# Loading the first expert group's up projection as whole matrices instead of quarters of four experts, in a one-core encoder kernel

## The chip, the core and the metric

The kernel runs on one core of one Trainium2 chip. It is written by hand, with explicit semaphores, for TensorE (PE in the profile), VectorE (DVE), ScalarE (ACT), GpSimd (POOL) and SyncE (SP), which here does little but issue DMA loads of weights. The metric is the device time of one execution in microseconds (us). Before the change it is 1241.25 us, the median of three runs (1240.59, 1241.25, 1242.27).

## The reference

A two-layer encoder trunk works on 256 tokens of width 1024, in float32. Each layer has a token mixer (neighbourhood attention in layer 0, gated linear attention in layer 1) beside a small memory attention, then an output projection, then a mixture of experts. The part that matters here is the mixture:

```
g_gate, g_idx = lax.top_k(g_prob, 1)             # one of 4 groups per token
top_l, top_i = lax.top_k(e_logits, TOP_K)        # two of its 8 experts
gate = softmax(top_l) * g_gate
...
def expert_block(args):
    xi, e = args
    return (jax.nn.silu(xi @ w1[e]) * (xi @ w3[e])) @ w2[e]
```

There are 32 experts in a layer. w1 and w3 of an expert are 1024 x 512, w2 is 512 x 1024, each 2 MB in float32. All of them are read in each layer, 192 MB a layer.

## The kernel before

**Groups of four experts.** The kernel walks the experts of a layer in 8 groups (NQ = 8) of four (E4 = 4), and gives each expert 32 rows of a 128-row tile. For each group `quad` on TensorE gathers the tokens by a matmul with a selection matrix (L644), multiplies them by w1 and then by w3 (both L657, the function `up`; m = 0 is w1, the "up projection" of the change, and m = 1 is w3), transposes the activation (L686), multiplies by w2 (L661, `down`) and adds the result back to the tokens (L712). Each float32 matmul is two instructions in the profile, so that w1 or w3 of one group is 64 rows on L657, and w2 is 64 rows on L661.

**The ring.** The weights go through a ring of 10 slots in SBUF, 2 MB each (SLOTS = 10). A group needs 12 fills: fills 0 to 3 for w1, 4 to 7 for w3, 8 to 11 for w2. SyncE issues the fills strictly in order (`experts` in the SyncE block, `load`, L434). Fills 0 to 9 of a layer go to slots that the mixer before has used, each behind its own condition (`free0`, `free1`). Fill n from the tenth on waits until TensorE has counted up `ring_used` for fill n - 10 (`free`, L422). So the last two fills of the first group, 10 and 11, which are half of its w2, go to the slots in which its fills 0 and 1 were. In the text "fill 10" means the eleventh fill of a layer.

**Two layouts of a fill.** If a matrix is "sliced" in a group, one fill holds a quarter of the rows of all four experts, in runs of 4 KB (tile 128x4x1024). If not, a fill is one expert's whole matrix, in runs of 16 KB (tile 128x4096). With sliced w1 TensorE waits for one fill, does 16 rows of matmul with it, counts `ring_used` up by one, and goes to the next. With whole w1 it waits for all four fills (L668), goes through all 64 rows with the four experts in turn, and counts the four fills as used at the last eight rows, where k is 7. The table `SLICED` says for each of the 8 groups which matrices are sliced, and holds for both layers:

```
SLICED = [(0,)] + [()] * (NQ - 2) + [(2,)]
```

The last group's w2 is sliced as well, and stays so.

Of the kernel before, what the change touches and what calls it, by code (L numbers as in the profile page):

```python
# [31 lines left out]
NQ = NE // E4  # L32
# [5 lines left out]
PAIRS = NQ // 2  # L38
KV_AT = 3
ORDER = ((1, 2, 3, 4, 5, 7, 8, 0, 6, 9), (3, 9, 0, 1, 2, 7, 8, 4, 6, 5))  # L40
SLICED = [(0,)] + [()] * (NQ - 2) + [(2,)]
LAPS = 2 * FILLS // XSLOTS
BIG = 1e30

# [35 lines left out]
def build(nc, x, mem, mem_norm, final_norm, norm_mix, norm_ffn, w_mem_kv, w_out, na_w_in, na_rpb, gla_w_in,  # L80
          gla_gate_up, gla_gate_bias, gla_out_norm, moe_w_group, moe_b_group, moe_w_router, moe_b_router,
          moe_w1, moe_w3, moe_w2, consts, out):
    with ExitStack() as ctx:
# [296 lines left out]
        def first_fill(l, g):  # L380

            return g * FILLS + (l == 0 and g >= KV_AT)
# [30 lines left out]
        def _(sp):  # L413
# [3 lines left out]
            def free(l, n):  # L417

                if n < SLOTS:
                    sp.wait_ge(*(free0, free1)[l][main[l].slots[n]])  # L420
                else:
                    sp.wait_ge(ring_used, main[l].used(0, n - SLOTS + 1))  # L422

            def load(rn, slot, l, g, f, sliced):

                w, i = f // 4, f % 4
                whole = (w1v, w3v, w2v)[w][l]
                if w in sliced:
                    dst = slot_view(slot).rearrange("p (e n) -> p e n", e=E4)
                    src = whole[:, bass.ds(g * E4, E4), i * 1024:i * 1024 + 1024]  # L430
                else:
                    dst = slot_view(slot).unsqueeze(1)
                    src = whole[:, bass.ds(g * E4 + i, 1), :]
                sp.dma_start(dst, src).then_inc(rn.ring_in[slot], 16)  # L434

            def experts(l):
                for g in range(NQ):
# [4 lines left out]
                    for f in range(FILLS):  # L442
                        free(l, n0 + f)
                        load(main[l], main[l].slots[n0 + f], l, g, f, SLICED[g])
                sp.wait_ge(rt_n[l], 1)
# [85 lines left out]
        def _(pe):  # L531
# [184 lines left out]
            def experts(l):  # L716
                for g in range(NQ):
                    if l == 0 and g == KV_AT:
                        mem_kv(1)
                        pe.wait_ge(kv_cp[1], 2)  # L720
                    quad(main[l], l * NQ + g, 0, first_fill(l, g), l * SELS + 2 * g + 1,
                         2 if g == NQ - 1 else 0, SLICED[g])
                if l == 0:
# [821 lines left out]
```

## Time and profile before

| what | value |
|---|---|
| median of three runs | 1241.25 us |
| the profiled execution's own time | 1241.44 us |
| its span in the trace | 1239.7 us |
| TensorE busy | 927.2 us (75%) |
| DMA moved | 444.06 MB, mean 358 GB/s over the span |
| DMA in the chain that ended last | 33% |

The span of the trace is 1.7 us shorter than the time of the same execution. Layer 0's experts run from about 170 to 626 us of the span, and layer 1's from about 779 us to 1230 us. A busy share is a mean over stages that have different limits; the stages are best read one by one, with the chain of waits and the windows.

### The profile page before, as it was taken

How to read it: one execution, taken by the hardware profiler on the slowest of the kernel's cores; microseconds unless marked ns; L12 is line 12 of the kernel's file. 1: busy time of each engine (PE TensorE's matmuls, PEld its weight loads, DVE VectorE, ACT ScalarE, POOL GpSimd, SP SyncE). 2: the span in 40 equal slices, each digit the busy share in tenths (PEclk: the TensorE clock that was granted, in tenths of full speed). 3: DMA queues.
4: the chain of work that ended last, by engine and by line, in shares of the span. 5: the costliest groups of instructions: out<-in, count | busy, mean ns of one | idle time of the engine just before them, and what ended most of it. 6: DMA issues, size and time to landing. Idle time of an engine off the chain costs nothing.

```text
span 1239.7 us, 12035 instructions
## 1 busy us (share of the span) xinstructions
PE 927.2 (75%) x5400; PEld 498.3 (40%) x5400; DVE 222.7 (18%) x371; ACT 146.7 (12%) x309; POOL 12.4 (1%) x9
## 2 busy tenths in 40 slices
PE   7999998574877483947789999975756666666656
PEld 5678454141544141414257655441413232322321
DVE  2234241010011010101036342310101010110111
ACT  2233210000000000000025321000000000000001
POOL 0300000000000000000000000000000000000000
PEclk9999999887888797969899999996979788888888
DMA  9973469999999999999995038799999999999992
GB/s 350 278 258 113 190 245 428 428 427 427 428 428 428 428 426 428 427 428 428 363 343 204 1 114 333 316 428 429 426 429 429 428 428 428 426 428 428 428 416 112
DMA packets 77209, 444.06 MB, mean 358 GB/s; under 512 B 31841, under 2 KB 41185, under 8 KB 54497
## 3 DMA queue, kind: packets, MB, share of 16 engines
q1 hardware_dynamic: 76288, 441.31, 87.1%
q10 hardware_dynamic: 864, 1.91, 0.4%
q8 instruction: 46, 0.75, 0.2%
q14 instruction: 11, 0.08, 0.0%
HBM read 442.15 MB, written 1.05 MB: 358 GB/s over the span
## 4 chain that ended last, share of the span: by engine, by line
PE 60%; DMA 33%; DVE 4%; ACT 2%; issue 1%; SPq 0%; DVEq 0%; ACTq 0%
DMA ring<-in_moe_w 32%; PE ps L661 11%; PE ps L657 11%; PE ps L644 9%; PE ps L575 5%; PE ps L611 4%; PE ps L712 4%; PE ps L775 3%; PE ps L838 2%; PE ps L538 1%; ACT work L1043 1%; PE ps L561 1%; PE ps L568 1%; PE ps L603 1%; PE ps L584 1%
## 5 line engine op out<-in xcount | busy, mean ns | idle before, releaser
L657 PE MATMUL ps<-ring,work 128*32 128x512 f32 x2048 | 252.8, 651 | 137.4 <-DMA ring<-in_moe_w 126.1
L661 PE MATMUL ps<-ring,work 128*32 128x512 f32 x1024 | 140.1, 704 | 110.9 <-DMA ring<-in_moe_w 109.5
L657 PEld LDWEIGHTS ps<-ring,work 128*32 128x32 f32 x2048 | 77.0, 119 | 302.4 <-issue 300.8
L644 PEld LDWEIGHTS ps<-work,xs 128*128 128x128 f32 x512 | 124.5, 335 | 6.9 <-issue 3.1
L644 PE MATMUL ps<-work,xs 128*128 128x128 f32 x512 | 123.5, 402 | 1.7 <-DVE work L1339 1.0
L661 PEld LDWEIGHTS ps<-ring,work 128*32 128x32 f32 x1024 | 37.7, 127 | 202.0 <-issue 200.3
L1366 DVE TENSOR_TENSOR xres<-xres,ps 128x1024 f32<-128x1024 f32 x32 | 39.1, 1221 | 341.4 <-PE ps L712 341.4
L712 PE MATMUL ps<-work 128*128 128x512 f32 x128 | 58.7, 602 | 19.5 <-ACT work L1043 19.5
L575 PE MATMUL ps<-ring 128*128 128x384 f32 x192 | 63.7, 490 | 0.0
L611 PE MATMUL ps<-ring 128*128 128x512 f32 x128 | 57.1, 596 | 0.0
L1363 DVE TENSOR_TENSOR work<-work,ps 128x512 f32<-128x512 f32 x16 | 11.0, 687 | 246.2 <-PE ps L657 246.2
L538 PE MATMUL ps<-cst 128*128 128x512 f32 x88 | 43.8, 630 | 7.0 <-DMA cst<-in_consts 5.7
L1043 ACT COPY work<-ps 128x512 f32<-128x512 f32 x32 | 17.2, 588 | 259.3 <-PE ps L661 259.3
L575 PEld LDWEIGHTS ps<-ring 128*128 128x128 f32 x192 | 36.0, 190 | 25.3 <-issue 1.8
L712 PEld LDWEIGHTS ps<-work 128*128 128x128 f32 x128 | 23.1, 190 | 56.3 <-issue 56.3
L775 PE MATMUL ps<-ring 128*128 128x256 f32 x192 | 43.0, 383 | 0.0
L1040 ACT COPY work<-ps 128x512 f32<-128x512 f32 x16 | 9.4, 586 | 282.1 <-PE ps L686 282.1
L1351 DVE TENSOR_TENSOR work<-ps,gcol 128x512 f32<-128x512 f32 x32 | 20.6, 686 | 113.7 <-PE ps L644 113.7
L775 PEld LDWEIGHTS ps<-ring 128*128 128x128 f32 x192 | 36.1, 190 | 6.7 <-issue 1.9
L611 PEld LDWEIGHTS ps<-ring 128*128 128x128 f32 x128 | 23.6, 191 | 26.8 <-issue 26.8
L1360 DVE TENSOR_TENSOR work<-work,ps 128x512 f32<-128x512 f32 x16 | 11.0, 688 | 103.8 <-ACT work L1038 103.8
L538 PEld LDWEIGHTS ps<-cst 128*128 128x128 f32 x88 | 16.0, 196 | 28.5 <-issue 21.1
(205 smaller groups left out, 578.6 us busy)
## 6 DMA issues: line engine op xcount, KB each, us to landing
ring<-in_moe_w SPq DMA_DIRECT2D x192, 2048.0 KB, 29.5
ring<-in_w_out SPq DMA_DIRECT2D x4, 2048.0 KB, 13.8
ring<-in_na_w_in SPq DMA_DIRECT2D x6, 1024.0 KB, 12.1
ring<-in_gla_w_in SPq DMA_DIRECT2D x1, 6144.0 KB, 19.8
ring<-in_na_w_in SPq DMA_DIRECT2D x1, 4096.0 KB, 19.7
ring<-in_na_rpb SPq DMA_DIRECT2D x12, 192.0 KB, 5.0
ring<-in_gla_w_in SPq DMA_DIRECT2D x6, 384.0 KB, 5.0
ring<-in_w_mem_kv SPq DMA_DIRECT2D x2, 1024.0 KB, 11.7
```

Source lines behind the costliest of these rows:

```text
L538: pe.matmul(ps[:, bank, :], ident, cst[:, 0:512], start=True, stop=True)
L575: t = pe.matmul(ps[:, bank, 0:384], hTs[l][:, k, a * P:(a + 1) * P], w[:, k, n0 + 384 * half:n0 + 384 * half + 384], start=k == 0, stop=k ...
L611: t = pe.matmul(ps[:, WOB[l][a] + half, :], mixTs[l][:, c, a * P:(a + 1) * P], wow[l][c // 4][:, c % 4, 512 * half:512 * half + 512], star ...
L644: t = pe.matmul(ps[:, k // 4, (k % 4) * P:(k % 4) * P + P], xs[:, a, k::KC], sel[:, a].rearrange("p e s -> p (e s)"), start=a == 0, stop=a ...
L657: return pe.matmul(ps[32 * e:32 * e + 32, 4 + m, :], xsel[:, k, 32 * e:32 * e + 32], w, start=k == 0, stop=k == KC - 1, tile_position=(0, ...
L661: return pe.matmul(ps[32 * e:32 * e + 32, 6 + half, :], actT[:, j, 32 * e:32 * e + 32], w, start=j == 0, stop=j == 3, tile_position=(0, 32 ...
L712: t = pe.matmul(ps[:, 4 + 2 * a + half, :], selwT[:, a, :], yb[:, half * 512:half * 512 + 512], start=True, stop=True)
L775: t = pe.matmul(ps[:, p % 2, t_ * T:(t_ + 1) * T], qkw[p][t_][:, k, :], hT0[:, k, :], start=k == 0, stop=k == KC - 1)
L838: t = pe.matmul(ps[:, 4 + j, t_ * T:(t_ + 1) * T], qkw1[t_][j][:, k, :], hT1[:, k, :], start=k == 0, stop=k == KC - 1)
L1043: nc.scalar.copy(yb[:, half * 512:half * 512 + 512], ps[:, 6 + half, :]).then_inc(rn.sig.yb_ready, 1)
L1351: V.tensor_tensor(xsel[:, 4 * b:4 * b + 4, :], ps[:, b, :].rearrange("p (k t) -> p k t", t=P), gcol[:, 2 + 2 * l, 4 * b:4 * b + 4].unsquee ...
L1366: V.tensor_tensor(xres[:, a, :], xres[:, a, :], ps[:, 4 + 2 * a:6 + 2 * a, :].rearrange("p b n -> p (b n)"), ALU.add).then_inc(rn.sig.adde ...
```

## The change

One entry of `SLICED` is removed, so that the first group of each layer is like the ones behind it. It holds for both layers. The last group keeps its sliced w2.

```diff
-SLICED = [(0,)] + [()] * (NQ - 2) + [(2,)]
+SLICED = [()] * (NQ - 1) + [(2,)]
```

In the queue of SyncE, layer 0, ahead of the experts, the rows are these before. `ring` is the ring in SBUF, `in_moe_w` the experts' weights, `pv_mm` and `logits0` stand for TensorE's progress in the attention and the router:

```order
 L483 DMA ring<-in_w_out 128x4x1024 [waits ring_used]
-L434 DMA ring<-in_moe_w 128x4x1024 [waits ring_used] x4
-L434 DMA ring<-in_moe_w 128x4096 [waits ring_used]
+L434 DMA ring<-in_moe_w 128x4096 [waits ring_used] x5
 L434 DMA ring<-in_moe_w 128x4096 [waits pv_mm] x2
 L434 DMA ring<-in_moe_w 128x4096 [waits ring_used] x2
```

The four fills of w1 stay in their place and in their number, and only their shape is another. In layer 1 the same four change in the same way.

On TensorE, in the first group of layer 0, just behind the gather and the transposes of L649, `ring_in1` to `ring_in4` are the arrival of the fills in slots 1 to 4 (fills 0 to 3), and `xsel_ready_first` is the gathered input from VectorE:

```order
-L657 MATMUL ps<-ring,work 32x512 [waits ring_in1,xsel_ready_first]
-L657 MATMUL ps<-ring,work 32x512 x7
-L657 MATMUL ps<-ring,work 32x512 [waits ring_in2]
-L657 MATMUL ps<-ring,work 32x512 x7
-L657 MATMUL ps<-ring,work 32x512 [waits ring_in3,xsel_ready_first]
-L657 MATMUL ps<-ring,work 32x512 x7
-L657 MATMUL ps<-ring,work 32x512 [waits ring_in4]
-L657 MATMUL ps<-ring,work 32x512 x7
+L657 MATMUL ps<-ring,work 32x512 [waits ring_in4,ring_in3,xsel_ready_first,ring_in2,ring_in1]
+L657 MATMUL ps<-ring,work 32x512 x15
+L657 MATMUL ps<-ring,work 32x512 [waits xsel_ready_first]
+L657 MATMUL ps<-ring,work 32x512 x15
```

The 32 matmuls (64 rows of the profile) stay, in the same order of k and of experts; the waits for the four fills move to the first of them. What the rows don't show is the count of `ring_used`: it stood at the end of each block of eight matmuls, and stands at the last four matmuls now. The other engines' instructions are the same.

## Rows read from the trace of the kernel before

**Rows 1.** The page, parts 2 and 4: DMA rate in 40 slices, chain by engine
```profile
GB/s 350 278 258 113 190 245 428 428 427 427 428 428 428 428 426 428 427 428 428 363 343 204 1 114 333 316 428 429 426 429 429 428 428 428 426 428 428 428 416 112
PE 60%; DMA 33%; DVE 4%; ACT 2%; issue 1%; SPq 0%; DVEq 0%; ACTq 0%
```

**Rows 2.** Chain of waits: start us, us, what
```profile
170.42 7.92 PE ps L644 x32
179.11 14.06 PE ps L657 x128
...
223.42 30.72 DMA ring<-in_moe_w
254.27 9.57 PE ps L661 x64
...
564.35 29.09 DMA ring<-in_moe_w
593.58 8.88 PE ps L657 x64
...
1166.25 30.22 DMA ring<-in_moe_w
1196.61 9.44 PE ps L657 x64
```

**Rows 3.** Windows: stretch, length, busy of five engines, clock, DMA share, GB/s
```profile
172.00:174.00 2.00, 2.00 (x10) 2.00 (x10) 1.37 (x7) 0.00 (x0) 0.00 (x0) 1.00 0.76 320
174.00:182.00 8.00, 7.43 (x49) 5.25 (x52) 2.05 (x4) 1.66 (x2) 0.00 (x0) 1.00 0.01 2
180.00:200.00 20.00, 18.37 (x172) 5.80 (x168) 1.80 (x3) 1.44 (x3) 0.00 (x0) 1.00 0.91 365
200.00:220.00 20.00, 17.91 (x106) 11.52 (x102) 4.49 (x6) 1.45 (x3) 0.00 (x0) 1.00 1.01 428
...
783.50:789.00 5.50, 4.93 (x32) 3.53 (x34) 2.05 (x4) 1.66 (x2) 0.00 (x0) 0.88 0.00 1
```

**Rows 4.** Timeline of SyncE: start us, us, issue of fills
```profile
181.09 0.33 SPq L434 DMA_DIRECT2D ring<-in_moe_w  x1
182.81 0.33 SPq L434 DMA_DIRECT2D ring<-in_moe_w  x1
...
223.05 0.33 SPq L434 DMA_DIRECT2D ring<-in_moe_w  x1
...
789.27 0.33 SPq L434 DMA_DIRECT2D ring<-in_moe_w  x1
...
831.23 0.80 SPq L434 DMA_DIRECT2D ring<-in_moe_w  x2
```

**Rows 5.** Timeline of TensorE: start us, us, line, idle before
```profile
195.43 7.07 PE L661 MATMUL ps<-ring,work 128*32 128x512 f32 x64 [0.68 <-ACT work L1040]
...
215.99 7.07 PE L657 MATMUL ps<-ring,work 128*32 128x512 f32 x64 [0.73 <-DVE work L1351]
...
234.03 9.34 PE L657 MATMUL ps<-ring,work 128*32 128x512 f32 x64 [10.96 <-DMA ring<-in_moe_w]
...
787.29 13.94 PE L657 MATMUL ps<-ring,work 128*32 128x512 f32 x128 [0.57 <-DVE work L1351]
...
824.17 7.07 PE L657 MATMUL ps<-ring,work 128*32 128x512 f32 x64 [0.73 <-DVE work L1351]
```

**Rows 6.** The page, part 6: DMA issues, KB each, us to landing
```profile
ring<-in_moe_w SPq DMA_DIRECT2D x192, 2048.0 KB, 29.5
```

**Rows 7.** Windows of the attention, with w1's fills, and of the last stream
```profile
88.00:93.00 5.00, 4.87 (x33) 3.90 (x33) 1.57 (x2) 1.66 (x3) 0.00 (x0) 1.00 1.02 410
...
103.00:108.00 5.00, 5.00 (x27) 4.09 (x28) 2.93 (x6) 2.24 (x8) 0.00 (x0) 1.00 0.93 372
...
113.00:118.00 5.00, 4.87 (x28) 3.96 (x27) 3.09 (x6) 2.01 (x9) 0.00 (x0) 1.00 0.00 0
...
1200.00:1205.00 5.00, 5.00 (x48) 1.65 (x44) 0.00 (x0) 0.00 (x0) 0.00 (x0) 0.88 1.03 410
```

## The prediction

> **What bounds the kernel now.** I read the page first. Its row of DMA rates stands at 426 to 429 GB/s from the seventh slice to the nineteenth, and again in layer 1, and is low or uneven in between; a third of the chain that ended last is DMA [rows 1]. So the kernel has two kinds of stages: the two mixers, in which DMA is often idle, and the two expert streams, in which it never is. The chain of waits, read next, says where the one passes into the other. In layer 0 it is TensorE work up to and with the first group's w1 and w3 (179.11 us), and from 223.42 us on there is a stretch of about 30 us in which it runs through DMA for every group, up to the last w3 of the layer at 593.58 us; in layer 1 the last such step ends at 1196.61 us [rows 2]. Between these points TensorE's own pace does not count, only when the stream started and how many bytes it carries. What follows the last landing (tail of the last group, and the next mixer) is TensorE's chain again and starts from that landing.
>
> The third view, the windows, shows when the stream starts. DMA falls off after 172 us and moves 2 GB/s from 174 to 182 us: the first ten fills are in, the ring is full, and SyncE stands at fill 10, whose slot the first group's w1 still holds [rows 3]. From 180 to 200 us it moves 365 GB/s x 20 us = 7.30 MB, which at 428 GB/s takes 17.06 us, so the data start at 200 - 17.06 = 182.94 us [rows 3]. After that there is no gap: 428 GB/s from 200 to 220 us, and in the page's slices all the way [rows 1, 3]. Layer 1 has the same hole, 1 GB/s from 783.5 to 789 us [rows 3].
>
> The fourth view is SyncE's own timeline. Fill 10 is issued at 181.09 us, 1.98 us after w1 started at 179.11 us, which is the end of the first quarter; fill 11 follows at 182.81 us [rows 2, 4]. In layer 1 it is 789.27 us against a start at 787.29 us, 1.98 us again [rows 4, 5]. So the first release in the first group's w1 is what starts each of the two streams.
>
> **The change, part by part.**
>
> (1) The release. With whole matrices no slot is free before the last eight of the 64 rows of w1. How long that takes needs no guess, since the second group's w1 is done in just this way: it starts at 215.99 us and SyncE issues the next fill at 223.05 us, 7.06 us later; in layer 1 824.17 and 831.23 us, 7.06 us [rows 4, 5]. The w1 of the first group has the same 64 rows, at full clock too. So fill 10 is issued 7.06 - 1.98 = 5.08 us later in each layer: at 186.17 us, and its data start at 182.94 + 5.08 = 188.02 us. From below, if the release came when the first of the four experts is done by count (row 58 of 64 at 0.109 us each, 13.94 us over 128 rows in rows 5), it would be 6.3 us and the delay 4.3 us; from above, if it waited for the very last row and the issue, 7.2 us and 5.2 us. I take 5.08, since it is the same code measured twice.
>
> (2) The stream cannot make this up. A fill is 2.097 MB, at 428 GB/s 4.90 us. DMA stands at its one full rate from the start to the end of the stream, fills lie queued (29.5 us from issue to landing, six fills' time) [rows 1, 6], and it carries as many bytes as before. A stream that starts 5.08 us later ends 5.08 us later, unless SyncE starves it anywhere. Before, fills 10 to 13 were issued one per quarter, 1.72 us apart, faster than DMA eats them; now all four come within 1.3 us (0.43 us each in SyncE's row), so that nothing starves there either.
>
> (3) The first group's w2. It needs fills 8 to 11, and 10 and 11 are the ones that are late. Fill 11 is through at 182.94 + 9.80 = 192.7 us before, and one more item is the time from the last byte to TensorE: fill 19 is through at 182.94 + 49.0 = 231.9 us, and w3 of the second group, which waits for it, starts at 234.03 us, 2.1 us later [rows 5]. So fill 11 was there at 194.8 us, just before w2 started behind ScalarE at 195.43 us [rows 5]. Now it is there at 188.02 + 9.80 + 2.1 = 199.9 us, and w2 starts 4.5 us late. Queued behind it on TensorE are the scatter, the second group's gather and its w1, which starts at 215.99 + 4.5 = 220.5 us; its own fill 15 is there at 188.02 + 29.4 + 2.1 = 219.5 us, so that adds nothing. Then w3 waits for fill 19 at 188.02 + 49.0 + 2.1 = 239.1 us; it waited 10.96 us before, to 234.03 us [rows 5], and this wait takes in the 4.5 us. VectorE and ScalarE only follow. The slots freed late are not missed: w2's are freed at about 207.4 us, when DMA has work up to fill 17, until 188.02 + 39.2 = 227.2 us; w1's of the second group at about 227.6 us, with work until 188.02 + 58.8 = 246.8 us. Were TensorE's clock to fall to half in the 4.5 us wait, w2 would take some 2 us more (9.34 against 7.07 us for 64 rows after an 11 us wait [rows 5]), still inside these margins of 19 us. Cost at nothing; without the cover it would be 4.5 us a layer.
>
> (4) The loads of w1 themselves. Runs of 4 KB seem slower: 410 GB/s in a full window with them at 88 us, and 410 GB/s at 1200 us, when the last w2 comes in quarters [rows 7]. At 428 a fill takes 4.90 us and at 410 5.11 us, so 0.2 us are saved per fill, 1.7 us for all eight. The last of the four is what DMA moves from 103 us on, and at 113 us DMA has nothing left to do, 66 us before the matmuls at 179 us [rows 7], so this is worth nothing. The wait for all four at the start costs nothing for the same reason. The Trainium skill, DMA: Bandwidth & Descriptors, section Specifications, gives 512 B as the smallest transfer for line rate; by that rule 4 KB and 16 KB runs move alike and even this saving would be none. The trace does not agree to the last few per cent (410 against 428 GB/s), and the sum is the same with either.
>
> **Sum.** Two layers by 5.08 us are 10.2 us. Against the profiled execution's own time, 1241.44 us (span 1239.7 us and 1.7 us around it), that is 1251.6 us; against the median of the runs, which is 0.2 us lower, 1251.4 us. I predict 1251.5 us.
>
> **Rivals.**
>
> A. The delay is hidden in one layer or in both, because the stream has slack that I don't see: 1246.5 us, or 1241.4 us. For it: the second group's w3 and w2 wait for DMA for long, which looks like slack. Against it: that is TensorE's slack, not DMA's, and DMA's rate leaves none [rows 1, 3].
>
> B. The late w2 adds to the late stream. Then each layer costs 5.08 + 4.5 us, 19.2 us in all, 1260.6 us. For it: the wait on TensorE is real. Against it: the 10.96 us wait behind it [rows 5]. It decides only if slots freed 4.5 us late starve DMA, and the margin is 19 us.
>
> C. The other side: the 16 KB runs bring more than the late release costs, 1.7 us saved and 1239.8 us. For it: 410 against 428 GB/s [rows 7]. It decides only if w1's fills land after their matmuls are ready, so that the stream is unbroken from them on. Against it: the hole in DMA's row from 174 us shows that the ring was full and waiting for TensorE [rows 3].
>
> D. Half of the release delay only: if TensorE's release in the first group came by count, as in the lower end of (1), 2 x 4.3 us, 1250.0 us.
>
> **Chances.** My case with D in it (1249.5 to 1253.5 us) 0.86. Rival A 0.07, of which 0.03 for both layers. Rival B in full or in part 0.05. Rival C 0.02. The range, 1248.5 to 1254.5 us, is the likeliest case with the bounds of (1) and some room for the profiled run not being the median one. A difference of 0.2%, 2.5 us, is about what a measurement of this kernel can tell from none. Faster 0.02, within it 0.03, slower 0.95.
>
> **What would show it.** In the changed profile SyncE issues fill 10 at about 186.2 us, and the hole in the DMA row is 13 us instead of 8; four issues follow each other closely. w1 and w3 of the first group still start at 179.1 us and take 14 us. L661 of the first group has 4 to 5 us of idle ahead of it, put down to DMA. The second group's w3 starts at 239.1 us, and all of layer 1 is moved by 5.1 us: its first w1 starts at 792.4 us, its last w3 at 1206.8 us. I am wrong if the second group's w3 starts later than the 5.1 us, if the moves in the two layers differ, or if the DMA rate dips behind the restart.

## The result, and the profile after

The changed kernel takes 1252.62 us (median of four runs, 1251.87 to 1255.82) against 1241.74 us for the kernel before in the same comparison (four runs). The ratio is 1.009, with a 95% interval of 1.0076 to 1.0103, so it is 9.4 to 12.8 us slower. The prediction was 1251.5 us, range 1248.5 to 1254.5 us. The profiled execution took 1251.97 us, with a span of 1250.2 us, which is 10.5 us more than before in both.

The page's rows that answer to [rows 1]. The DMA row has lost rate in the sixth slice (205 against 245 GB/s) and in the twenty-sixth (248 against 316 GB/s), which is where the two streams start. The seventh slice still has a little of it (415 against 428 GB/s); elsewhere in the two streams the rates are the same to about 1%:

```profile
GB/s 349 277 265 108 180 205 415 427 430 426 428 427 428 428 427 428 427 427 428 364 337 205 1 122 330 248 428 429 427 427 428 428 428 428 428 426 428 427 418 119
PE 58%; DMA 34%; DVE 3%; ACT 2%; issue 1%; SPq 0%; DVEq 0%; ACTq 0%
ring<-in_moe_w SPq DMA_DIRECT2D x192, 2048.0 KB, 29.6
```

The chain of waits after, to be read against [rows 2] (start us, us, what):

```profile
170.67 7.94 PE ps L644 x32
179.47 7.17 PE ps L657 x64
186.90 12.86 DMA ring<-in_moe_w
199.90 9.16 PE ps L661 x64
...
229.86 29.95 DMA ring<-in_moe_w
259.94 9.85 PE ps L661 x64
...
570.28 28.78 DMA ring<-in_moe_w
599.19 9.19 PE ps L657 x64
...
793.29 7.17 PE ps L657 x64
800.72 12.64 DMA ring<-in_moe_w
813.50 9.56 PE ps L661 x64
...
1178.47 29.36 DMA ring<-in_moe_w
1207.97 8.59 PE ps L657 x64
```

Before, the chain went through all 128 rows of the first group's w1 and w3. Now it leaves TensorE at the end of w1 (x64, 7.17 us) and goes on with a DMA: the load that this end has released, and for which the first group's w2 waits.

The windows show the hole in the DMA row. It began at 174 us in both kernels, and reaches to 187 us now, where it reached to 182 us in [rows 3]:

```profile
174.00:187.00 13.00, 12.35 (x94) 7.44 (x97) 2.05 (x4) 1.99 (x3) 0.00 (x0) 0.90 0.01 3
...
180.00:200.00 20.00, 14.26 (x136) 5.31 (x132) 2.06 (x4) 1.71 (x3) 0.00 (x0) 0.93 0.64 252
200.00:220.00 20.00, 18.64 (x99) 10.28 (x99) 2.44 (x2) 1.07 (x2) 0.00 (x0) 0.90 1.00 428
```

Between 180 and 200 us DMA moves 5.04 MB, 11.78 us' worth at 428 GB/s, so the data start at 188.22 us, 8.75 us after w1's start at 179.47 us. Before it was 182.94 - 179.11 = 3.83 us. The difference is 4.92 us.

SyncE's timeline has the release itself, in layer 0 and then in layer 1 (answering to [rows 4]):

```profile
186.53 0.81 SPq L434 DMA_DIRECT2D ring<-in_moe_w  x2
...
800.35 1.98 SPq L434 DMA_DIRECT2D ring<-in_moe_w  x4
```

The first is 186.53 - 179.47 = 7.06 us after w1 starts, the second 800.35 - 793.29 = 7.06 us. Before it was 1.98 us in both.

TensorE's timeline of the first two groups, to be read against [rows 5]:

```profile
179.47 13.94 PE L657 MATMUL ps<-ring,work 128*32 128x512 f32 x128 [0.66 <-DVE work L1351]
...
199.90 9.04 PE L661 MATMUL ps<-ring,work 128*32 128x512 f32 x64 [4.81 <-DMA ring<-in_moe_w]
...
222.43 7.07 PE L657 MATMUL ps<-ring,work 128*32 128x512 f32 x64 [0.73 <-DVE work L1351]
239.15 9.89 PE L657 MATMUL ps<-ring,work 128*32 128x512 f32 x64 [9.65 <-DMA ring<-in_moe_w]
```

w2 waits 4.81 us for DMA, where before it had started behind ScalarE, and the second group's w3 starts at 239.15 us, 5.12 us later than before.

To compare kernels stream by stream, the length used from here on is the one from the start of the first group's w1 to the start of the last group's w3, both on TensorE. Before it is 593.58 - 179.11 = 414.47 us in layer 0 and 1196.61 - 787.29 = 409.32 us in layer 1 [rows 2, 5]; after it is 599.19 - 179.47 = 419.72 us and 1207.97 - 793.29 = 414.68 us. The span's 10.5 us are then: 0.36 us ahead of the first stream, 5.25 us in it, 0.39 us between the streams, 5.36 us in the second, and -0.86 us behind it.

### The profile page after: what moved, and what is told of

Read it like the earlier page. It is cut to its first block, busy times and chain, and to the rows that moved or that the text cites. A ratio compares the mean times of both kernels' runs of the same rounds, so it can differ in the third digit from the quotient of the medians.

```text
span 1250.2 us, 12035 instructions
## 1 busy us (share of the span) xinstructions
PE 931.4 (75%) x5400; PEld 500.6 (40%) x5400; DVE 222.3 (18%) x371; ACT 146.8 (12%) x309; POOL 12.4 (1%) x9
## 4 chain that ended last, share of the span: by engine, by line
PE 58%; DMA 34%; DVE 3%; ACT 2%; issue 1%; SPq 0%; DVEq 0%; ACTq 0%
DMA ring<-in_moe_w 34%; PE ps L661 12%; PE ps L657 9%; PE ps L644 9%; PE ps L575 5%; PE ps L611 4%; PE ps L712 4%; PE ps L775 3%; PE ps L838 2%; PE ps L538 1%; ACT work L1043 1%; PE ps L561 1%; PE ps L568 1%; PE ps L603 1%; PE ps L584 1%
## 5 line engine op out<-in xcount | busy, mean ns | idle before, releaser
L657 PE MATMUL ps<-ring,work 128*32 128x512 f32 x2048 | 251.3, 648 | 135.5 <-DMA ring<-in_moe_w 124.0
L661 PE MATMUL ps<-ring,work 128*32 128x512 f32 x1024 | 145.9, 729 | 118.8 <-DMA ring<-in_moe_w 118.8
L657 PEld LDWEIGHTS ps<-ring,work 128*32 128x32 f32 x2048 | 78.2, 118 | 297.9 <-issue 297.9
L661 PEld LDWEIGHTS ps<-ring,work 128*32 128x32 f32 x1024 | 39.3, 131 | 214.1 <-issue 214.1
L538 PE MATMUL ps<-cst 128*128 128x512 f32 x88 | 43.7, 628 | 7.3 <-DMA cst<-in_consts 5.9
L538 PEld LDWEIGHTS ps<-cst 128*128 128x128 f32 x88 | 16.0, 196 | 28.8 <-issue 21.1
```

The source lines that it names most:

```text
L538: pe.matmul(ps[:, bank, :], ident, cst[:, 0:512], start=True, stop=True)
L657: return pe.matmul(ps[32 * e:32 * e + 32, 4 + m, :], xsel[:, k, 32 * e:32 * e + 32], w, start=k == 0, stop=k == KC - 1, tile_position=(0, ...
L661: return pe.matmul(ps[32 * e:32 * e + 32, 6 + half, :], actT[:, j, 32 * e:32 * e + 32], w, start=j == 0, stop=j == 3, tile_position=(0, 32 ...
```

## The experiments

Theory 1 is the prediction's: the first release in the first group's w1 starts a stream that DMA bounds from end to end, and moves all of it. "First issue" in the table is SyncE's issue of fill 10 after w1's start, in layer 0. The two lengths are those defined above, each out of one profiled execution.

| kernel | first issue | length, layer 0 | length, layer 1 | ratio to before (95%) | median us |
|---|---|---|---|---|---|
| before | 1.98 | 414.47 | 409.32 | | 1241.9 to 1242.7 |
| the change again | 7.06 | 419.67 | 414.88 | 1.0077 (1.0058 to 1.0096) | 1252.85 |
| whole in layer 0 only | 7.05 | 419.44 | 409.60 | 1.0039 (1.0025 to 1.0053) | 1247.40 |
| whole in layer 1 only | 1.98 | 414.64 | 414.80 | 1.0053 (1.0037 to 1.0069) | 1248.44 |
| quarters, released last | 7.13 | 420.23 | 414.93 | 1.0082 (1.0058 to 1.0106) | 1253.36 |
| quarters, released in pairs | 3.70 | 416.25 | 411.56 | 1.0031 (1.0020 to 1.0043) | 1245.78 |
| w2 late only | 1.99 | 414.70 | 409.70 | 1.0007 (0.9999 to 1.0016) | 1242.85 |
| half fill first | 1.13 | 414.29 | 409.18 | 1.0004 (0.9996 to 1.0013) | 1243.89 |

Layers that one of these edits leaves alone come out 0.2 to 0.4 us longer than in the profile of before. The noise of a length is larger than that, as the kernels at the end of this section show. Two of them differ from before and from the change only by work in the last group, and their lengths are 0.5 to 1.0 us shorter than their sisters'. In layer 0 the difference is there long before the added work: from w1's start to the second group's w2 it is 254.27 - 179.11 = 75.16 us before, and 254.38 - 179.90 = 74.48 us in the kernel with that work. So a single length is good to about 1 us.

**The change again.**

> The changed kernel itself beside the others, so that its parts are compared in the same rounds. Both theories: about 1252 us, +10 to 11 us.

It was measured at +0.77%, 1252.85 us. Its profiled run, 1255.61 us, is the slowest of its four, and is taken up below.

**The release without the layout.**

```diff
-                            t.then_inc(rn.ring_used, 1)
+                            if f == 3:
+                                t.then_inc(rn.ring_used, 4)
```

> The loads of the kernel before (quarters of four experts, 4 KB runs, TensorE starts on each as it lands), but the four fills are counted as used together, at the end of the first group's w1. Theory 1, the time of the first release starts the stream: SyncE issues fill 10 some 7.1 us after w1 starts instead of 1.98 us, and the time is that of the change, +10.2 us, about 1252 us. Rival, the layout (run length, the wait for all four fills) makes the difference: no change, about 1241.5 us.

Every load has the shape it had before, and the whole cost is there (1253.36 us, and both streams as long as in the changed kernel to within 0.6 us). TensorE's w2 waits in the same way as after the change:

```profile
199.93 9.10 PE L661 MATMUL ps<-ring,work 128*32 128x512 f32 x64 [5.05 <-DMA ring<-in_moe_w]
```

So the cost is the time of the release, and neither the run length nor the wait for four fills. The rival is refuted. The runs of 16 KB do move faster, and the time doesn't show it. From 84 to 92 us, while layer 0's w1 is loaded, DMA moves 426 to 430 GB/s in the three profiles with whole matrices there (the change twice, and the change in layer 0 only), and 408 to 409 GB/s in four with quarters (before, layer 1 only, and the two other releases).

**Layer by layer.**

```diff
+SLICED = [[()] + [()] * (NQ - 2) + [(2,)], [(0,)] + [()] * (NQ - 2) + [(2,)]]   # indexed by layer
```

> The change in layer 0 alone. Theory 1: each stream is moved by its own release, 5.1 us here, about 1246.7 us, and layer 1 is only displaced. Rival A, slack in one of the layers: 0 or 10 us for this half.

> The change in layer 1 alone. Theory 1: 5.1 us, about 1246.7 us, and the two halves add up to the whole. Rival A: the one half costs all, the other nothing.

Each stream is longer only where its own first group is whole, by 4.8 us in the one and 5.2 us in the other against the same stream left alone in the sister kernel. The medians are 5.5 and 6.5 us above before, with intervals of 3.1 to 6.6 and 4.6 to 8.6 us; the expected 5.1 us lies in both, and their sum of 12.0 us within the 9.4 to 12.8 us of the whole. Rival A, slack in one layer, is refuted.

**A release half as late.**

```diff
-                            t.then_inc(rn.ring_used, 1)
+                            if f % 2:
+                                t.then_inc(rn.ring_used, 2)
```

> Quarters as before, but counted as used two at a time: the first release comes after 32 rows of w1 instead of 16, 3.7 us after its start instead of 1.98 us. Theory 1, a straight line through release time: 2 x 1.72 = 3.4 us, about 1245 us. Rival, a late release costs only once a whole set of four is late (a threshold): no change.

The first issue is at 183.11 us, 3.70 us after w1 starts at 179.41 us, and the streams are 1.8 and 2.2 us longer than before; the whole is 0.31% slower (2.5 to 5.3 us), where 3.4 us were expected. So there is no threshold: 3.70 us already costs, about a microsecond of stream for each of release.

**The late w2 without the late release.**

```diff
                 pe.wait_ge(rn.sig.actT_ready, c + 1)
+                if 0 in sliced:
+                    keep_warm(5, 2)
```

> The kernel before with 5 spare matmuls (about 4.5 us of TensorE) ahead of the first group's w2 in both layers, nothing else: the late w2 of the change without its late release. Theory 1: the second group's w3 waits for DMA anyway, its wait of 11 us gets 3.8 to 4.5 us shorter, no change of the time. Rival B, the late w2 adds to the late stream: +7.6 to 9 us, about 1250 us.

TensorE in layer 0, the spare matmuls being over at 200.16 us:

```profile
200.16 7.07 PE L661 MATMUL ps<-ring,work 128*32 128x512 f32 x64
...
220.72 7.08 PE L657 MATMUL ps<-ring,work 128*32 128x512 f32 x64 [0.73 <-DVE work L1353]
234.15 9.85 PE L657 MATMUL ps<-ring,work 128*32 128x512 f32 x64 [6.36 <-DMA ring<-in_moe_w]
```

w2 is 4.7 us late, as in the change, and the wait ahead of the second group's w3 shrinks from 10.96 us [rows 5] to 6.36 us; w3 starts 54.81 us after w1's start, against 54.92 us before. The time moves by -0.1 to +2.0 us, where rival B wanted at least 7.6. Rival B is refuted. w2 takes 7.07 us here and not the 9.04 us of the change, so the 2 us of a cold w2 are not in this test; the 6.36 us of wait that are left would cover them.

**An earlier release still.**

```diff
+                        if (g, f) == (0, SLOTS):
+                            sp.wait_ge(half_used, l + 1)      # signalled after 8 rows of w1
...
+                            sp.dma_start(half[:, :, 0:FF], src[:, :, 0:FF]).then_inc(half_in, 16)
+                            free(l, n0 + f)
+                            sp.dma_start(half[:, :, FF:2 * FF], src[:, :, FF:2 * FF]).then_inc(ring_in[slot], 16)
```

> The kernel before, with the first release moved forward: TensorE signals after the first 8 rows of w1 that the half of the quarter it has used is free, and SyncE loads the first half of fill 10 there (1 MB in 2 KB runs), the other half when the quarter is done. Theory 1: the first issue comes 1.1 us after w1 starts instead of 1.98 us, 0.87 us a layer, 1.7 us faster, about 1239.8 us. Rival, the start is bound by something else than the release, or the 2 KB runs cost as much: no change or slower by up to 1 us.

SyncE does issue earlier, at 180.47 us, 1.13 us after w1's start at 179.34 us. In the window from 180 to 200 us DMA moves more than before (376 against 365 GB/s):

```profile
180.00:200.00 20.00, 18.37 (x171) 5.67 (x167) 2.02 (x4) 1.67 (x3) 0.00 (x0) 1.00 0.93 376
```

By the same reckoning as for the other kernels the data start at 182.43 us, 3.09 us after w1's start instead of 3.83, a gain of 0.74 us. The second group's w3 starts 54.30 us after w1's start, against 54.92 us. But the streams at their end are shorter by only 0.2 us and 0.1 us than in the profile of before (0.3 to 0.5 us than in the other kernels that leave them alone), and the time does not move. The lead shrinks at the very next wait: the second group's w2 starts 254.25 - 179.34 = 74.91 us after w1, against 75.16 us before, and 74.48 to 75.43 us in kernels that start the stream as before does. So 0.7 us at one landing is within what these landings vary by, and what became of it can't be told from one profile. My expectation was too high; the interval of the time leaves out the 1.7 us that it asked for.

**The clock at the end of a stream.** The spread between runs of one kernel asked for an explanation. In the second profile of the change (1255.61 us) the distance from the last w3 of layer 0 (599.06 us) to the first w1 of layer 1 (795.57 us) is 196.51 us, where it is 194.10 us in the first (599.19 to 793.29 us) and 193.71 us before. Its chain there, with w3, and the two spare matmuls (L538) ahead of the last w2:

```profile
599.06 9.95 PE ps L657 x64
...
611.27 3.60 PE ps L538 x4
```

The same rows take 9.19 and 1.98 us in the first profile of the change, and these two differences are 2.38 of the 2.41 us. The windows of the kernel before say what happens ahead of them: TensorE stands still for 9 us, its granted clock falls to the lower level, 1.2 GHz (0.50), and w3 begins at that:

```profile
589.60:593.50 3.90, 0.00 (x0) 0.00 (x0) 0.00 (x0) 0.00 (x0) 0.00 (x0) 0.50 0.98 398
593.50:595.50 2.00, 1.92 (x12) 0.68 (x16) 0.00 (x0) 0.00 (x0) 0.00 (x0) 0.50 1.02 408
```

In the other groups such a slow start is covered by the next DMA wait, as the second group's w3 is (9.34 us, then 9.21 us of wait ahead of its w2, before); in the last one no such wait follows. So I filled the wait ahead of the last w3 with work, in both kernels:

```diff
+                    if m == 1 and 2 in sliced:
+                        keep_warm(9, 3)
                     ws = [landed(4 * m + e) for e in range(E4)]
```

> The kernel before with 9 spare matmuls (8.0 us of TensorE) in the last group of each layer, between its w1 and its w3, where TensorE waited 9.05 and 10.18 us for DMA. Theory 2, TensorE's clock at the end of a stream makes the spread of the runs and part of what is above the 10.2 us: w3 takes 7.2 us instead of 8.9 and 9.4 us, the spare matmuls ahead of w2 are never cold, so about 4 us faster, 1238.5 us, and the runs lie closer together. Rival, the clock there is covered by DMA: no change.

> The same spare matmuls in the changed kernel, so that nothing but the late release differs from the run beside it. Theory 1 with 2: 10.2 us above that run, about 1248.7 us, 6 to 7 us above the kernel before. Rival, part of the cost of the change is the clock: less than 9.5 us above it.

> The spare matmuls together with the first half fill that is loaded after 8 rows of w1. If the clock hid the gain of the half fill: 0.6 to 1.7 us below the run with the spare matmuls alone. If the half fill brings nothing to the end of the stream: the same.

On the kernel before it gives 1237.0 us, ratio 0.9961 (0.9947 to 0.9975), 3.1 to 6.6 us faster: the fastest version of this study. w3 takes its 7.07 us in both layers (layer 0 here):

```profile
584.75 7.99 PE L538 MATMUL ps<-cst 128*128 128x512 f32 x18
593.77 7.07 PE L657 MATMUL ps<-ring,work 128*32 128x512 f32 x64 [1.02 <-DMA ring<-in_moe_w]
```

Two parts of the expectation did not come true. The spare matmuls ahead of w2 were to be never cold; in layer 1 they are:

```profile
1203.97 2.83 PE ps L538 x4
```

So the low clock was in part only moved. And the runs don't lie closer together: 1236.54 to 1241.92 us, where the kernel before has 1241.37 to 1244.40 us in the same comparison. In the profiled run (1238.84 us) the span is 2.7 us shorter than before; 1.70 us of that are between the streams and 0.64 us behind the second, which is what the clock gives there. The other 0.4 us are the streams, shorter by 0.60 and 0.55 us, which is within what a length varies by, against a start that is 0.79 us later. That the clock makes up all of the 5.5 us between the medians is not shown.

On the changed kernel it gives 1250.49 us, ratio 1.0058 (1.0045 to 1.0071). The medians are 13.5 us apart from its partner's; the two ratios are 12.1 us apart, with intervals wide enough for 10.2 us. In the two profiled runs, 13.2 us apart, the excess can be traced. Its streams are 4.87 and 5.37 us longer than the partner's (418.74 against 413.87, 414.14 against 408.77 us), 10.2 us as expected. The rest is between the streams, 195.42 against 192.01 us, and is the clock again. In layer 0 the spare matmuls ended 2.17 us ahead of the landing, and w3 takes 1.70 us and the spare matmuls behind it 1.41 us more than in the partner. The clock was still at 1.00 in that gap, and 0.50 from 600 us on, inside w3:

```profile
588.04 7.99 PE L538 MATMUL ps<-cst 128*128 128x512 f32 x18
598.21 8.77 PE L657 MATMUL ps<-ring,work 128*32 128x512 f32 x64 [2.17 <-DMA ring<-in_moe_w]
...
609.33 3.39 PE L538 MATMUL ps<-cst 128*128 128x512 f32 x4 [0.68 <-ACT work L1042]
```

```profile
596.00:598.20 2.20, 0.03 (x1) 0.02 (x1) 0.00 (x0) 0.00 (x0) 0.00 (x0) 1.00 0.98 397
598.20:600.00 1.80, 1.79 (x16) 0.70 (x20) 0.00 (x0) 0.00 (x0) 0.00 (x0) 0.87 1.03 412
600.00:602.50 2.50, 2.50 (x16) 0.81 (x12) 0.00 (x0) 0.00 (x0) 0.00 (x0) 0.50 1.02 406
```

In layer 1, after a gap of 1.56 us, w3 had its full clock, and the spare matmuls behind it took 3.68 us:

```profile
1217.19 3.68 PE ps L538 x4
```

A fixed number of spare matmuls thus doesn't hold the clock in every case. The kernel with the half fill as well took 1238.75 us, ratio 0.9972 (0.9961 to 0.9983). Its interval overlaps that of the one without it, and their profiled spans are equal (1237.0 us both), so no gain of the half fill shows here either.

## Why the prediction was right

**Step 1, the release.** 5.08 us later was predicted, from the second group's w1. In the trace it is 7.06 us after w1's start in both layers against 1.98 us, exactly that. Rival D, a release by count at row 58 of 64, did not show: the issue comes only 0.07 us ahead of that of the kernel which counts all four fills at row 64 (7.13 us). Why it does not come earlier is open; the step held because it took the same code's measured time and not the count. The layout alone had no part in it, as the release in quarters at the end showed. The hole in the DMA row is 13 us instead of 8, as forecast.

**Step 2, the stream cannot make it up.** Over the profiles at hand, leaving out those with spare matmuls ahead of the last w3, whole first groups have mean lengths of 419.61 us in layer 0 and 414.79 us in layer 1 (three profiles each) and quartered ones that are released as before, the late w2 among them, 414.60 and 409.54 us (three each): 5.01 and 5.25 us, 10.3 us in sum, against a predicted 10.2 us. With about 1 us of noise in a single length, agreement to 0.1 us is partly luck.

**Step 3, w2.** w2 was to start at 199.9 us and did at 199.90 us, after a wait of 4.81 us. The second group's w3 was to start at 239.1 us and did at 239.15 us. That w2 costs nothing was shown with the late w2 alone. Its clock did fall, as the step allowed for: 9.04 against 7.07 us, inside the cover.

**Step 4, the loads.** The 16 KB runs are faster by about what the step took from the rows, 426 to 430 against 408 to 409 GB/s, and they are worth nothing, as said. The 1.7 us of rival C never had a place: with the late release and the old layout the time was the same as that of the change.

**The start of layer 1.** I forecast its first w1 at 792.4 us and its last w3 at 1206.8 us; they were at 793.29 and 1207.97 us. The 0.9 us by then are 0.36 us ahead of the first stream, 0.17 us in it above 5.08 and 0.39 us between the streams.

**What the sum missed.** The medians are 10.9 us apart, 0.7 us more than predicted; the interval of 9.4 to 12.8 us holds both. What varies from run to run, beside the streams' own 1 us, is TensorE's clock at their ends, which no step of the prediction named: 196.51 against 194.10 us between the streams in two profiles of the same kernel. That it makes up the 0.7 us is not shown.

## What to carry to other kernels

In a ring that is filled ahead of a DMA-bound stream, the first slot's release sets when the stream starts. Here, between 2 and 7 us, every microsecond of it was paid in full, while no gain showed from a release earlier than that, and the releases behind a w2 that was 4.7 us late had slack. So in such a ring the first consumer should take its data in the order that frees a slot soonest, even if that means shorter runs (as long as these land early enough, here 66 us ahead), and the cost of another order can be read from two rows: the time from the first matmul to the first issue, as it is, and where the other order is already in use. And where the same stream ends, the consumer that has been waiting starts with a cold clock, and here nothing behind it covered that.

## What the runs showed of the hardware that I had not expected

In the kernel before, TensorE, idle for 9 us ahead of the last w3, had a granted clock of 0.50. In the nine profiles without spare matmuls there, after 8.6 to 10.2 us of idle, the 64 rows took 8.5 to 10.2 us in the chain, where they take 7.17 us at 1.00. The two spare matmuls behind it took 1.98 us in most of these nine, and 3.40 and 3.60 us in two, in layer 0.

In the kernels with spare matmuls, the clock stayed at 1.00 in a gap of 2.17 us and fell to 0.50 only inside the work that followed. And w3 at its full clock did not mean that the next matmuls had it: the two spare ones behind it then took 2.83, 2.93 and 3.68 us in layer 1 of three kernels.
